# Four normalizations in which the second weight panel's two parts are made before the squares and the root instead of after them

## The reference

```python
x = x + 0.5 * swiglu(rms_norm(x, ffn1_norm), ...)          # n1, ffn1
h = rms_norm(x, mix_norm); z = h @ w_in                    # nm, mixer
x = x + m @ w_out                                          # m: gated gMLP and differential attention
x = x + 0.5 * swiglu(rms_norm(x, ffn2_norm), ...)          # n2, ffn2
h = _rms(x, norm1_w) * (1 + sc1) + sh1; proj = h @ w_in_2  # p1, mix2
x = x + g1 * (mixed @ w_out_2)                             # mixed: _rms of S5 (ps) and of attention (pa)
h2 = _rms(x, norm2_w) * (1 + sc2) + sh2                    # p2
x = x + g2 * _conv_ffn(h2, w_up, conv_w, conv_b, w_down)   # ffn3
```

## Time and profile before

| what | value |
|---|---|
| three runs, median (lowest, highest) | 1959.64 us (1957.53, 1962.68) |
| the profiled execution's own time | 1957.97 us |
| its span, first to last instruction | 1956.1 us |
| mean granted clock of PE | 0.985 of 2.4 GHz |
| PE busy | 1874.0 us, 96% |
| DVE busy | 1122.3 us, 57% |
| ACT busy | 764.0 us, 39% |
| POOL busy | 249.3 us, 13% |
| HBM traffic | 102 GB/s over the span |

### The profile page before, as it was taken

One profiled execution on the slowest core, in us unless ns is written; L12 is line 12 of the kernel. 1 busy time (PEld: TensorE's weight loads), 2 busy tenths in 40 slices (PEclk: granted clock), 3 DMA queues, 4 the chain that ended last, 5 costly groups with the idle time before them and its releaser, 6 DMA issues.

```text
span 1956.1 us, 22665 instructions
## 1 busy us (share of the span) xinstructions
PE 1874.0 (96%) x8169; PEld 1443.9 (74%) x8169; DVE 1122.3 (57%) x1447; ACT 764.0 (39%) x1077; POOL 249.3 (13%) x241
## 2 busy tenths in 40 slices
PE   8999999999999999999999999997787999999998
PEld 5888888878886778777888888684334768888887
DVE  6566336354555566548777333548998566556533
ACT  4222222243346866224444322333324354455422
POOL 2112001100000000031100000304674300000000
PEclk9999999999999999999999999999998999999999
DMA  6555313233221121235545222432110222223222
GB/s 203 194 172 183 117 60 105 94 115 106 87 86 65 44 65 65 87 107 179 186 141 170 86 86 91 129 108 75 54 54 11 86 65 93 100 86 95 74 88 86
DMA packets 161895, 200.57 MB, mean 103 GB/s; under 512 B 7104, under 2 KB 136490, under 8 KB 161834
## 3 DMA queue, kind: packets, MB, share of 16 engines
q1 hardware_dynamic: 148714, 163.02, 26.2%
q0 software_dynamic: 8672, 28.33, 4.4%
q10 hardware_dynamic: 4448, 8.41, 1.1%
HBM read 189.24 MB, written 10.50 MB: 102 GB/s over the span
## 4 chain that ended last, share of the span: by engine, by line
PE 87%; DVE 9%; ACT 2%; issue 2%; DMA 0%; POOL 0%; DVEq 0%; POOLq 0%; ACTq 0%
PE bank L1674 40%; PE bank L1641 34%; PE bank L1857 6%; DVE sc_a L1523 2%; PE bank L1616 2%; PE bank L1881 1%; DVE sc_v L1532 1%; PE bank L1653 1%; PE bank L1766 1%; DVE tmp L1544 1%; DVE sc_p L1544 1%; PE bank L2069 1%; DVE sc_p L1543 1%; DVE tmp L1028 1%; PE bank L1892 0%
## 5 line engine op out<-in xcount | busy, mean ns | idle before, releaser
L1012 DVE TENSOR_TENSOR w_lo<-w_raw,w_hi 128x2048 fp32r<-128x2048 f32 x157 | 369.7, 2355 | 466.3 <-ACT w_hi L615 466.1
L615 ACT CAST w_hi<-w_raw 128x2048 fp32r<-128x2048 f32 x158 | 301.3, 1907 | 757.7 <-PE bank L1674 367.5
L1674 PE MATMUL bank<-h_hi,w_hi 128*128 128x512 f32 x1120 | 448.7, 401 | 19.4 <-ACT h_hi L638 9.3
L1674 PE MATMUL bank<-h_hi,w_lo 128*128 128x512 f32 x1120 | 445.5, 398 | 0.0
L1674 PE MATMUL bank<-h_lo,w_hi 128*128 128x512 f32 x1120 | 355.3, 398 | 0.1
L1674 PEld LDWEIGHTS bank<-h_hi,w_hi 128*128 128x128 f32 x1120 | 212.6, 190 | 74.4 <-issue 22.8
L1674 PEld LDWEIGHTS bank<-h_lo,w_hi 128*128 128x128 f32 x1120 | 212.0, 189 | 52.1 <-DVE h_lo L1038 0.5
L1674 PEld LDWEIGHTS bank<-h_hi,w_lo 128*128 128x128 f32 x1120 | 212.7, 190 | 50.2 <-issue 0.2
L1641 PE MATMUL bank<-hid_hi,w_lo 128*128 128x512 f32 x528 | 208.8, 396 | 0.0
L1641 PE MATMUL bank<-hid_hi,w_hi 128*128 128x512 f32 x528 | 208.8, 396 | 0.0
L1641 PE MATMUL bank<-hid_lo,w_hi 128*128 128x512 f32 x528 | 208.8, 396 | 0.0
(11 more groups left out here) (368 smaller groups left out, 2590.6 us busy)
## 6 DMA issues: line engine op xcount, KB each, us to landing
w_raw<-in_w_in SPq DMA_DIRECT2D x29, 1024.0 KB, 5.2
mod_raw<-in_w_mod POOLq DMA_DIRECT2D x96, 256.0 KB, 3.6
w_raw<-in_ffn_w_gate SPq DMA_DIRECT2D x22, 1024.0 KB, 6.8
w_raw<-in_ffn_w_up SPq DMA_DIRECT2D x22, 1024.0 KB, 5.4
w_raw<-in_w_up SPq DMA_DIRECT2D x22, 1024.0 KB, 5.1
w_raw<-in_ffn_w_down SPq DMA_DIRECT2D x16, 768.0 KB, 4.6
w_raw<-in_ffn_w_down SPq DMA_DIRECT2D x16, 640.0 KB, 4.3
w_raw<-in_w_out SPq DMA_DIRECT2D x8, 1024.0 KB, 5.1
```

What stands on the lines that cost most here:

```text
L615: act.copy(w_hi[i % 2][:], w_raw[i % 2][:]).then_inc(S("w_hi_done"), 1)
L1012: dve.tensor_tensor(w_lo[s][:], w_raw[s][:], w_hi[s][:].bitcast(F32), ALU.subtract).then_inc(S("w_split"), 1)
L1674: mm = pe.matmul(bank[:], w[:, k, at], h[:, k, :], start=k == first and part == 0 and i == 0, stop=k == last and part == 1)
```

## The change

At nm, n2, p1 and p2 both engines make their part of `panel` at the head of the normalization: ACT before it waits for the last two tiles of x and squares them, DVE before it waits for the root. The later places, after the root on ACT and at k == 5 on DVE, are then skipped, since `panel` is None. n1 keeps its order. Instructions, operands and waits are the same; their order on ACT and DVE is not.

```diff
 ACT, norm():
                 count, direct = NORM_PARTS[name]
+                if panel is not None and name != "n1":
+                    split(panel)
+                    panel = None
                 for d in range(direct if ready else 0):
                     if d in between:
                         split(between[d])
 DVE, norm():
                 eps = eps_width_col[width]
+                if panel is not None and name != "n1":
+                    split(panel)
+                    panel = None
                 dve.wait_ge(S("norm_root"), NORMS.index(name) + 1)
                 done(dve.scalar_tensor_tensor(v, B[7][:], eps, rstd[:], ALU.add, ALU.mult))
```

## The result

| | before | after |
|---|---|---|
| median of 7 runs | 1959.64 us (1957.53 to 1963.17) | 1966.23 us (1963.89 to 1967.82) |
| ratio | | 1.0031, 95% interval 1.0020 to 1.0043 |
| profiled execution, its span | 1957.97, 1956.1 us | 1964.93, 1963.3 us |

The change made the kernel slower by 6.1 us by the ratio (3.9 to 8.4), 6.6 by the medians. The forecast was 1967.8, range 1963.0 to 1971.5, so direction and range held. The likeliest case, 8.1 us, was too high by 1.5 to 2. Whether it is more than 0.3% (5.9 us) stays undecided: the interval has room on both sides.

A forecast was written before the change was run, and what follows sets the result against it. PE, busy 96% of the span, was taken to bound the kernel, so time changes only where it waits. Root 7.6 plus POOL 0.8 minus DVE 0.3 gave 8.1 us longer: median 1967.8 us, range 1963.0 to 1971.5.

The forecast's parts named there:

- Where ACT is put, and the root: At four normalizations: cast at S+0.05 (S: start of last piece of x), root at S+4.56, 7.6 us later in all.
- The drain: At the table load before the root: no drain seen; by the skill's 2.66 us, about 6.8 us in place of 7.6.
- DVE's split under the root's cover: Ahead of DVE's wait for the root: over at about S+4.3, root ends S+5.25; costs nothing, cover 1 us thick.
- POOL's select at nm: At nm, POOL's select on ws_in would fall on DVE's steps on rstd: 0.8 us, could be nothing or 1.5.
- At the other sites PE goes through that stretch without a gap: In DVE's loop after the fifth tile: 2.2 us freed, worth 0.27 us at p1; 0.3 us taken back for all.
- The clock: Behind the four starts PE runs slow for 17.8 us, half, 8.9 us, lost; the change alters this by zero.
- Rival 2: At the four sites, sums split the pause, PE starts at 2.4 GHz, 8.9 us come back: 1958.8; chance 0.07.
- Rival 3: Cast runs in ACT's idle time, root stays where it was; only DVE's 0.3 us return: 1959.3; chance 0.05.
- Rival 4: Split's cover breaks: POOL holds DVE more than 1 us at each site; 2 us in all, 1969.8; chance 0.04.

The follow-up runs named there:

- Run 2: Changed kernel with ACT's cast between the two squares, not ahead of both: 1964.71 us, ratio 1.0030 to the kernel before.
- Run 6: Kernel before with only DVE's split moved ahead of its wait for the root, ACT's cast still behind the root: 1974.83 us, ratio 1.0082.
- run 7: Changed kernel with POOL's select on ws_in held back until all eight tiles of nm are split: 1965.08 us, ratio 1.0033 to the kernel before.
- run 3: Kernel before plus 18 unused products on PE behind the sums of the four normalizations: 1958.53 us, ratio 1.0000 to the kernel before.
- run 4: Changed kernel plus 18 unused products on PE behind the sums of the four normalizations: 1960.68 us, ratio 1.0005 to the kernel before.
- run 8: Kernel before plus 18 spare products and DVE's split behind its loop at nm, p1, p2, POOL's select held back: 1954.46 us, ratio 0.9979.

## Why the prediction was right or wrong

- **Where ACT is put, and the root.** Right. Cast at S+0.05, root at S+4.56 (four sites, 4.56 forecast). Run 2 confirms its two parts, the cast and the sum that lost its cover: with one sum covered again the root is 0.76 to 0.86 us earlier, the full 0.86 where no table load stands beside it.
- **The drain.** The Trainium skill ("ScalarE: Activation LUTs", What ACT_TABLE_LOAD costs) adds a drain to the load. In run 2 the table load starts at 405.85 and the root at 407.15, 1.30 us later, so here too no drain shows. The 6.8 us that the prediction works out by that figure count a load at all four sites; p2 has none, so it would be about 7.0.
- **DVE's split under the root's cover.** Right, 1.00 us thick as said. Run 6 shows what it costs when the cast is not ahead of the root: cast and split both stand in the chain, 15.5 us in all.
- **POOL's select at nm.** Right in place and nearly in size: 0.94 us on a step on rstd, 0.8 forecast, shown by run 7. By the rule of the Trainium skill ("SBUF — State Buffer", Who interferes with whom) at its harshest, the select's whole length, it would be 1.09 us as the select now runs. The trace's 0.94 lies close to it and above what I took.
- **The step that failed** is "At the other sites PE goes through that stretch without a gap", with "I take 0.3 us back for all four; it could be nothing, or 0.3 at each of the three sites". It followed DVE only to the end of its loop over the tiles. At n2 DVE goes straight into the angles and the modulation, and PE waited 1.24 us for its split 34 us behind S, in a trace where I had that wait before me and did not ask whose lateness it was. The site costs nothing that can be measured, where 1.9 stood in the sum: DVE's late start is paid by the 2.2 us won in its loop, and PE's by the 1.24 us that it had to spare, together with 0.95 of a better clock there. With 1.9 taken out the sum is 6.2, and 6.1 was measured by the ratio. That it is so near is luck in part, since neither the interval (3.9 to 8.4) nor the sites are that sharp. The range held because it was wide enough for a term of 1.9 us that was not there.
- **The clock.** "I take zero" was right for the change as a whole: the mean granted clock over whole executions is the same. In the profiles it is 15.1 slow microseconds against 17.8, 1.3 us given back, with 1.9 us less at n2 and 3.1 less at p2, and 2.0 more at p1. Run 2 shows that the order of the same work can move it. What was loose is the price. Half the slow time is lost only where PE is the late engine; runs 3 and 4 removed all of it and got back nothing and 4.7 us.
- **The rivals.** Rival 2, that PE keeps the clock, is refuted: it started slow at all four sites. Rival 3, a cast in ACT's idle time, too: every cast waits for PE. Rival 4 is refuted, the cover held. The rival that came true in part, DVE bound in the stage behind a normalization, was none of mine.

## What to carry to other kernels

Work that can't start before an event is not moved into the idle time ahead of that event by writing it earlier; it goes to the head of the queue at the event, in front of whatever else waits for it. Before moving it, ask what each engine behind it does for the next 40 us and not only until the next meeting point: an engine that is late there gives a moved piece of work its price. And when a cost is a slow clock, fill the pause only where nobody else is late, or the time comes back as a wait.

## What the runs showed of the hardware that was not expected

The clock fell behind short waits. In run 8 PE waited 1.25 us for w_lo, and from 901 to 910 us its granted clock was 0.83; in the kernel before the same wait of 1.24 us left it at 1.00. In run 3 two waits of 1.40 and 0.93 us within 3 us were followed by a granted clock of 0.77 over 15 us. So a single wait of this size can cost nothing or another microsecond and a half, and two profiles of one stage can differ by that much. Eighteen spare products, 4.2 us of a pause that lasts 4.5 to 5.4 us without them, kept PE at 2.4 GHz behind all eleven starts (runs 3, 4 and 8), at no visible cost to the root.
